# Local attention in a two-layer decoder trunk: the second pair's scores move behind the first pair's, into other banks

## What is computed

```
s = q @ k.T * 64**-0.5          # per head, causal blocks only: 128x128 and 128x256
m = max over the allowed keys
p = count * exp(s - m)          # count: in how many of the three windows a key lies
o = (p / sum(p)) @ v
```

## Time and profile before

| | |
|---|---|
| median of 3 runs | 818.95 us (818.94 to 819.08) |
| the profiled execution | 818.96 us |
| its span in the profile | 816.8 us |
| PE busy | 808.3 us, 4636 matmuls |
| DVE busy | 654.4 us |
| ACT busy | 528.0 us |
| weights and inputs read | 143.87 MB |

### The profile page before, as it was taken

How to read it: one execution, slowest core, us unless ns; L and a number is a source line. 1 busy time by engine, 2 the same in 40 slices (tenths; PEclk the granted TensorE clock), 3 DMA queues, 4 the chain that set the end, 5 groups by cost and what they waited for, 6 DMA issues and landing times.

```text
span 816.8 us, 12147 instructions
## 1 busy us (share of the span) xinstructions
PE 808.3 (99%) x4636; PEld 697.9 (85%) x4636; DVE 654.4 (80%) x1149; ACT 528.0 (65%) x823; POOL 29.3 (4%) x54
## 2 busy tenths in 40 slices
PE   8999999999999999999999999999999999999997
PEld 5998888889888888888899889888988888888885
DVE  6899996777776899997387999948788489999753
ACT  6656886568557777765365589656766477776441
POOL 2100000010010000000010000001000000000000
PEclk9999999999999999999999999999999999999999
DMA  8755345472564566556567443456635545655651
GB/s 304 280 183 179 104 129 169 142 261 98 161 246 138 156 205 203 182 186 218 192 202 237 148 155 106 136 173 204 208 111 198 182 130 181 199 178 190 226 186 52
DMA packets 40446, 145.72 MB, mean 178 GB/s; under 512 B 4594, under 2 KB 4738, under 8 KB 40388
## 3 DMA queue, kind: packets, MB, share of 16 engines
q1 hardware_dynamic: 38448, 138.38, 52.1%
q0 software_dynamic: 1936, 6.55, 2.4%
q10 hardware_dynamic: 4, 0.00, 0.0%
HBM read 143.87 MB, written 1.05 MB: 177 GB/s over the span
## 4 chain that ended last, share of the span: by engine, by line
PE 90%; DVE 5%; ACT 3%; issue 1%; DMA 0%; DVEq 0%; POOLq 0%; POOL 0%; ACTq 0%
PE acc L1686 8%; PE psCD L1686 4%; PE acc L1652 4%; PE acc L1654 4%; PE acc L1653 4%; PE acc L1696 4%; PE acc L1749 4%; PE psAB L1686 4%; PE acc L1751 4%; PE acc L1750 4%; PE psAB L1654 3%; PE psAB L1652 3%; PE psAB L1653 3%; PE psCD L1599 3%; PE acc L1669 3%; PE acc L1670 2%
## 5 line engine op out<-in xcount | busy, mean ns | idle before, releaser
L996 DVE TENSOR_TENSOR wlo<-raw,whi 128x1024 fp32r<-128x1024 f32 x240 | 288.0, 1221 | 68.3 <-ACT whi L569 66.7
L569 ACT ACTIVATE whi<-raw 128x1024 fp32r<-128x1024 f32 x240 | 249.4, 1057 | 121.1 <-PE acc L1654 44.1
L1686 PE MATMUL acc<-xT,whi 128*128 128x512 f32 x288 | 89.0, 390 | 0.0
L1686 PEld LDWEIGHTS acc<-xT,whi 128*128 128x128 f32 x288 | 54.1, 188 | 11.8
L1540 DVE SCALAR_TENSOR_TENSOR KT<-V,par,KT 128x255 f32<-128x255 f32 (+1 forms) x144 | 59.9, 479 | 2.1 <-ACT KT L929 1.5
L1696 PE MATMUL acc<-xT,wlo 128*128 128x256 f32 x288 | 58.0, 283 | 0.0
L1669 PE MATMUL acc<-xT,whi 128*128 128x256 f32 x176 | 50.9, 289 | 0.0
L1276 DVE SCALAR_TENSOR_TENSOR arena<-arena,par 128x256 f32<-128x256 f32 x120 | 50.2, 479 | 0.8 <-ACT arena L769 0.8
L1686 PE MATMUL psCD<-xT,whi 128*128 128x512 f32 x160 | 50.0, 393 | 0.0
L1670 PE MATMUL acc<-xT,whi 128*128 128x256 f32 x176 | 49.7, 283 | 0.0
L1671 PE MATMUL acc<-xT,wlo 128*128 128x256 f32 x176 | 49.7, 282 | 0.0
(11 more groups left out here) (336 smaller groups left out, 2083.7 us busy)
## 6 DMA issues: line engine op xcount, KB each, us to landing
raw<-stream_dram SPq DMA_DIRECT2D x256, 512.0 KB, 4.1
gpost<-gain_dram POOLq DMA_DIRECT2D x6, 512.0 KB, 5.2
gpre<-gain_dram POOLq DMA_DIRECT2D x5, 512.0 KB, 5.8
memn<-mem_dram SPq DMA_DIRECT2D x2, 512.0 KB, 10.1
out_dram<-h SPq DMA_DIRECT2D x4, 256.0 KB, 2.0
cst<-const_dram SPq DMA_DIRECT2D x1, 896.0 KB, 6.3
h<-x_dram SPq DMA_DIRECT2D x2, 256.0 KB, 2.8
h<-x_dram SPq DMA_DIRECT2D x1, 512.0 KB, 7.7
```

The costliest lines, as they stand in the source:

```text
L569: act.activation(home(g)[0], raw[:, s * GW:(s + 1) * GW], ACT.Copy).then_inc(w_hi.sem, 1)
L996: dve.tensor_tensor(lo, raw[:, cols], hi.bitcast(F32), ALU.subtract).then_inc(w_lo.sem, 1)
L1686: e = pe.matmul(up_halves(j, c), whi[:, cols], both, start=k == 0, stop=k == KC - 1)
```

## The change

The second pair's scores go to the banks `psCD` instead of `psAB`, directly behind the first pair's on PE and with no wait. `scores_max` reads them there. On DVE the second pair's maxima and then the first pair's probabilities go ahead of a split that stood between the first pair's maxima and probabilities. The third pair's scores wait for the first pair's maxima instead of the second's (same banks `psAB`), the fourth's for the third's as before. The first flip gets one more wait per head: for the second pair's maxima, since it writes the banks that they are read from. ACT's order is not touched.

```diff
+        score_banks = lambda c: psCD if c == 1 else psAB
...
-                            e = dve.tensor_tensor_reduce(sms[c % 2][r][:, a:b], psAB[r][:, a:b], negm[:, a:b], 1.0,
+                            e = dve.tensor_tensor_reduce(sms[c % 2][r][:, a:b], score_banks(c)[r][:, a:b], negm[:, a:b], 1.0,
                                                          -3e38, ALU.add, ALU.max, st(S_MX + w + 2 * r + q))
...
                 split(G_DLV + 3 + AHEAD)
                 dve.wait_ge(cst_in.sem, 16)
                 scores_max(0)
+                scores_max(1)
+                probabilities(0)
                 split(G_SBQK + AHEAD)
-                probabilities(0)
-                scores_max(1)
                 split(G_SBQK + 1 + AHEAD)
                 probabilities(1)
                 scores_max(2)
...
                 def dl_scores(c):
                     for r in range(2):
-                        if c:
-                            pe.wait_ge(nb_ready.sem, nb_ready.at(l, 2 * (c - 1) + r + 1))
+                        if c >= 2:
+                            pe.wait_ge(nb_ready.sem, nb_ready.at(l, 2 * (0 if c == 2 else 2) + r + 1))
                         q, k = (a[r * HD:(r + 1) * HD, c, :] for a in (dqT, dkT))
-                        pe.matmul(psAB[r][:, 0:P], q[:, 0:P], k[:, 0:P], start=True, stop=True)
-                        pe.matmul(psAB[r][:, P:AW], q[:, P:SEQ], k, start=True, stop=True).then_inc(s_done.sem, 1)
+                        bank = score_banks(c)[r]
+                        pe.matmul(bank[:, 0:P], q[:, 0:P], k[:, 0:P], start=True, stop=True)
+                        pe.matmul(bank[:, P:AW], q[:, P:SEQ], k, start=True, stop=True).then_inc(s_done.sem, 1)
 
                 def dl_flip(c):
                     for r in range(2):
+                        if c == 0:
+                            pe.wait_ge(nb_ready.sem, nb_ready.at(l, 2 + r + 1))
                         pe.wait_ge(p_ready.sem, p_ready.at(l, 2 * c + r + 1))
                         flip(psCD[r], sms[c % 2][r], 3).then_inc(p_tr.sem, 1)
...
                 dl_scores(0)
+                dl_scores(1)
                 transposed_product(G_SBQK, 1, X, acc[0])
-                dl_scores(1)
                 transposed_product(G_SBQK + 1, 1, X, acc[0], k0=2)
                 dl_flip(0)
                 dl_scores(2)
```

## The result

The changed kernel takes 820.28 us (median of 21 runs) against 818.91 us of the kernel before (21 runs beside it). The ratio is 1.0016, 95% interval 1.0010 to 1.0022: slower by 0.8 to 1.8 us. The difference of the medians, 1.37 us, is under the 1.64 us (0.2%) that the prediction took as the bound of "same", though the upper end of the interval is not; the median lies inside the predicted range of 818.5 to 820.6 us. The profiled execution took 820.18 us with a span of 818.1 us.

A forecast was written before the change was run, and what follows sets the result against it. Bound in each layer by PE up to local attention's last flip, then by ACT's time in its chain with DVE; 2 x 0.41 = +0.82 us on 818.96 gave 819.8 us, range 818.5 to 820.6.

The forecast's parts named there:

- PE's saved waits come back at the first flip: First flip: PE arrives earlier, but 0.5 us (layer 0) and 1.4 us (layer 1) turn into waits for probabilities.
- Pair 0 is scaled 0.68 us later: ACT's scaling: on DVE 1.82 us of maxima replace a 1.14 us split, so ACT's wait grows from 1.00 to 1.68.
- Nothing takes it up on the way: ACT's rows behind the scaling: none waits for PE, so 0.68 us travels unchanged through the third and fourth pair.
- The third pair's scores at 0.05 us earlier than before: PE behind the flip of head 1: third pair's scores start at 80.87 against 80.92, with 0.05 for the semaphore.
- 0.41 us per layer reaches the chain: PE's stick-breaking scores start at 96.07 instead of 95.66, 0.41 us later, carried unchanged to 123.22; layer 1 repeats it.
- The two sides agree, which is why the number can be trusted: Hand-over at the last flip: ACT free at 100.43, PE's side 100.48, within 0.05; ACT alone would bring 0.36.
- The new wait costs nothing in this order: First flip's wait on the second pair's maxima: free, as they precede pair 0's probabilities; at most 1.77 us without that.
- The reading by busy share: Taking the engine with highest occupancy as the one to relieve: PE's shorter waits would count in full, 1.69 us.
- PE keeps what it saves: PE's shorter waits at the scores count, 1.69 us saved (between 1.37 and 2.23): 817.3 us; chance 0.05.
- The delay is taken up: Slack in the loop of ACT and DVE: each layer between 0 and -0.32, 818.3 to 819.0 us; chance 0.17.
- The whole delay and more: 0.68 us arrives in each layer: 820.3, or 820.7 us with 0.2 extra hand-over in each; chance 0.09.
- The granted clock: PE's clock falls to 1.2 GHz after idling before the first flip, doubling a 2.87 us product: 825.5 us; chance 0.03.

The follow-up runs named there:

- the two delays: Kernel before with two, then three, extra DVE products ahead of pair 0's probabilities: 820.95 and 822.24 us, against 818.97.
- the banks alone: Changed kernel's PE order and banks, with DVE's order as in the kernel before: 819.71 us against 818.97, ratio 1.0010.
- the doubled delay: Kernel before with three extra DVE products of 384 columns ahead of pair 0's probabilities: 822.24 us against 818.97, ratio 1.0039.
- the balanced order and the old banks: Kernel before, scores unmoved; DVE order: maxima 0, split formerly ahead of them, probabilities 0, maxima 1, other splits; 817.62 us, ratio 0.9989.

## Why the prediction was right

- **PE's saved waits come back at the first flip:** right. The second block of scores cost 0.76 us (taken: 0.7), and layer 1's saving turned into waits of 0.85 and 0.22. The 0.85 counts from the end of the last matmul's record; from the moment at which the next one would have started, as the prediction counts, it is 1.00, where 0.9 or more was the sign.
- **Pair 0 is scaled 0.68 us later:** right, 0.70 and 0.69, and ACT's wait of 1.68 in layer 0 was met to the hundredth (1.75 in layer 1). DVE's wait of about 0.7 at the second split is 0.70.
- **Nothing takes it up on the way:** right, and shown by the two delays, with 0.89 us of time for 0.88 of delay.
- **The third pair's scores at 0.05 us earlier than before:** wrong by a little. From PE's first scores they came 81.34 - 72.56 = 8.78 us later, before 80.92 - 72.28 = 8.64, so 0.14 late. ACT's scaling ends at 80.25 + 0.50 = 80.75 and PE's flip of head 1 starts at 80.89, 0.14 later instead of 0.05; the flip then took 81.34 - 80.89 = 0.45 instead of 0.37.
- **0.41 us per layer reaches the chain:** the direction right, the size short: 0.55. The mis-sized term is the hand-over from ACT to PE. I took "some 0.05 for the semaphore". ACT's copy ends at 95.25 + 1.09 = 96.34, and PE starts the stick-breaking scores at 96.48, 0.14 later; the chain shows the same 0.14 as "issue" before the values of pair 2. So the slack that I read as 0.33 - 0.05 = 0.28 us was only about 0.15 to 0.19. The rest, some 0.05, is that the delay grew a little along ACT's chain: 23.78 us from the first scores to the end of that copy, against 23.05, is 0.73. Against the start of the first maxima the stick-breaking scores came 0.53 us late, where the sign said some 0.4.
- **The two sides agree, which is why the number can be trusted:** they did not come out within 0.05 of each other. ACT was free at 99.91 + 0.85 = 100.76 and took PE's last flip at 100.88, 0.12 later, so PE's side alone set the time.
- **The new wait costs nothing in this order:** right here; the cover named for it, the maxima being early, is what the run with the banks alone took away, at 0.36 us per layer.
- **The reading by busy share:** PE is "99% busy" in both kernels, and 0.9 us of it less (808.3 to 807.4) came with a longer time. The busy share doesn't tell here what the time does; the chain of waits does.
- **The rivals:** "PE keeps what it saves" fell with the banks alone (+0.73 us, where it needed -1.4 or better). "The delay is taken up" fell with the delays. "The whole delay and more" was the nearest, at 0.55 of 0.70 per layer. The granted clock stayed at 1.00 through the idle time of 0.85 us. Of the chances, "slower" should have been 0.06 (0.03 and a third of 0.09) rather than 0.07; nothing hangs on it.

The sum of the two stages, 1.10 us, lies in the timed interval (0.8 to 1.8).

## What to carry to other kernels

Moving work ahead in one engine's order moves everything behind it back: what went ahead of the first pair's probabilities here was no longer a 1.14 us split but 1.8 us of maxima nobody was yet waiting for. Before removing a wait of the busiest engine, look along the chain for the next thing that engine needs, and ask who makes it and whether that comes earlier too. When a reordering loses, dummy instructions at the suspected place, in two lengths that are read from the trace, show whether the place is on the chain and how much slack it has.

## What the runs showed of the hardware that was not expected

- The hand-over from ACT's last row to PE's first waiting matmul is 0.14 us at the stick-breaking scores (0.20 with the doubled delay); I had allowed 0.05. From DVE to PE it is 0.05: in the run with the banks alone DVE's row ends at 80.40 + 0.17 = 80.57, and the flip that waits for it starts at 80.62.
- The time at which PE reaches local attention in layer 0 differs between the profiled executions, one of each kernel, although the work ahead of it is the same: 72.56 us in the changed kernel, 72.28 before, and 71.44 in the run with the balanced order and the old banks (its row on PE follows).

```profile
71.44 0.50 PE L1797 MATMUL psAB<-arena 64*128 64x128 f32 x4
```

That spread of about 1 us is as large as the whole effect; comparing two spans would have misled, and lengths taken from a mark inside the stage did not.
